# Fetched token rows turned in the odd groups' banks, ahead of the last up product, in a mixture-of-experts kernel

## The reference

```python
D_MODEL = 1024; SEQ = 256; N_EXPERTS = 8; TOP_K = 2; D_FF_EXPERT = 3584

def swiglu(x, wg, wu, wd):
    return (jax.nn.silu(x @ wg) * (x @ wu)) @ wd

def moe_swiglu(xn, router, wg, wu, wd):
    t = xn.reshape(B * S, D)
    logits = (t @ router).astype(jnp.float32)
    top_val, top_idx = lax.top_k(logits, TOP_K)
    gates = jax.nn.softmax(top_val, axis=-1)
    combine = jnp.sum(jax.nn.one_hot(top_idx, N_EXPERTS) * gates[..., None], axis=1)
    out = jnp.zeros_like(t)
    for e in range(N_EXPERTS):
        out = out + combine[:, e:e + 1] * swiglu(t, wg[e], wu[e], wd[e])
    return out
```

## Time and profile before

| what | value |
|---|---|
| median of three runs | 1982.92 us (1981.67 to 1983.06) |
| the profiled execution's own time | 1982.62 us |
| its span in the profile | 1980.8 us |
| mean granted TensorE clock | 0.993 of full speed |
| TensorE busy with matmuls | 97% of the span |
| VectorE busy | 77% |
| ScalarE busy | 62% |
| expert stage | about 517 to 1486 us of the span |

### The profile page before, as it was taken

The page is one execution under the profiler, slowest core; times in us unless marked ns, Lnnn a source line. Parts: engine busy times, 40 slices in busy tenths (PEclk is TensorE's granted clock), DMA queues, the critical chain, the costliest instruction groups (busy, mean ns, idle before and its releaser), DMA issues.

```text
span 1980.8 us, 26870 instructions
## 1 busy us (share of the span) xinstructions
PE 1923.5 (97%) x10275; PEld 1632.1 (82%) x10275; DVE 1518.7 (77%) x1478; ACT 1229.4 (62%) x1332; POOL 28.4 (1%) x28
## 2 busy tenths in 40 slices
PE   8999999999899999999999999999998999999999
PEld 7889998887687887878878788787886788887987
DVE  4675555656788888888888888888996865877576
ACT  4554445554677777777777777777776545354442
POOL 0000000000000000000000000000000000000000
PEclk9999999999999999999999999999999999999999
DMA  7717554532799999999999999999995552345321
GB/s 240 255 59 249 188 192 149 164 113 99 280 375 341 391 379 348 381 340 390 379 348 373 361 395 374 359 384 353 396 361 203 170 171 86 128 170 191 128 86 43
DMA packets 246211, 514.63 MB, mean 260 GB/s; under 512 B 12516, under 2 KB 59240, under 8 KB 246120
## 3 DMA queue, kind: packets, MB, share of 16 engines
q1 hardware_dynamic: 242936, 502.77, 70.4%
q0 software_dynamic: 2896, 10.49, 1.3%
q10 hardware_dynamic: 288, 0.11, 0.0%
HBM read 507.56 MB, written 5.77 MB: 259 GB/s over the span
## 4 chain that ended last, share of the span: by engine, by line
PE 81%; DVE 10%; ACT 3%; issue 3%; SPq 2%; DMA 1%; DVEq 0%; ACTq 0%
PE bank L725 25%; PE bank L727 25%; PE bank L726 25%; DVE low L1936 3%; PE bank L1145 1%; DVE low L2533 1%; PE bank L696 1%; PE bank L849 1%; ACT high L1417 1%; SPq L674 1%; SPq L635 1%; DVE at L2738 1%; PE bank L840 1%; ACT high L1620 1%; PE bank L818 1%
## 5 line engine op out<-in xcount | busy, mean ns | idle before, releaser
L2533 DVE TENSOR_TENSOR low<-raw,high 128x2048 fp32r<-128x2048 f32 x336 | 768.4, 2291 | 117.7 <-ACT high L1620 116.8
L1620 ACT ACTIVATE high<-raw 128x2048 fp32r<-128x2048 f32 x336 | 644.7, 1920 | 240.1 <-PE bank L727 238.3
L1936 DVE TENSOR_TENSOR low<-raw,high 128x2048 fp32r<-128x2048 f32 (+1 forms) x138 | 310.5, 2259 | 168.1 <-ACT high L1417 164.4
L1417 ACT ACTIVATE high<-raw 128x2048 fp32r<-128x2048 f32 (+1 forms) x138 | 260.7, 1894 | 167.8 <-PE bank L727 150.3
L725 PE MATMUL bank<-high,xg_hi 128*128 128x512 f32 x896 | 353.7, 395 | 2.7 <-DVE xg_lo L2516 2.3
L727 PE MATMUL bank<-high,xg_lo 128*128 128x512 f32 x896 | 349.5, 390 | 0.0
L726 PE MATMUL bank<-low,xg_hi 128*128 128x512 f32 x896 | 348.9, 389 | 0.0
L725 PE MATMUL bank<-high,xT_hi 128*128 128x512 f32 (+1 forms) x576 | 228.3, 396 | 8.5 <-issue 5.4
L727 PE MATMUL bank<-high,xT_lo 128*128 128x512 f32 (+1 forms) x576 | 222.2, 386 | 0.0
L726 PE MATMUL bank<-low,xT_hi 128*128 128x512 f32 (+1 forms) x576 | 221.8, 385 | 0.0
L725 PE MATMUL bank<-high,hT_hi 128*128 128x512 f32 x536 | 212.7, 397 | 0.0
(11 more groups left out here) (346 smaller groups left out, 2231.5 us busy)
## 6 DMA issues: line engine op xcount, KB each, us to landing
raw<-in_moe_w_gate SPq DMA_DIRECT2D x112, 1024.0 KB, 6.5
raw<-in_moe_w_up SPq DMA_DIRECT2D x112, 1024.0 KB, 6.8
raw<-in_moe_w_down SPq DMA_DIRECT2D x112, 1024.0 KB, 6.6
raw<-in_w_in SPq DMA_DIRECT2D x63, 1024.0 KB, 5.4
raw<-in_w_out SPq DMA_DIRECT2D x20, 1024.0 KB, 5.0
raw<-in_dense_w_gate SPq DMA_DIRECT2D x11, 1024.0 KB, 5.2
raw<-in_dense_w_up SPq DMA_DIRECT2D x11, 1024.0 KB, 5.3
raw<-in_dense_w_down SPq DMA_DIRECT2D x11, 1024.0 KB, 5.0
```

Of the source, the lines that this page charges most:

```text
L1417: act.activation(high[:, slot, 0:k * n], raw[:, raw_slot[piece], 0:k * n], ACT.Copy).then_inc(high_done, 1)
L1620: act.activation(high[:, k % PARTS, :], raw[:, slot, :], ACT.Copy).then_inc(s["high"], 1)
L1936: dve.tensor_tensor(low[:, slot, 0:k * n], src, high[:, slot, 0:k * n].bitcast(F32), ALU.subtract).then_inc(low_done, 1)
L2533: dve.tensor_tensor(low[:, k % PARTS, :], raw[:, at0 + k % slots, :], high[:, k % PARTS, :].bitcast(F32), ALU.subtract).then_inc(s["low"], 1)
```

## The change

In the pass that fetches rows by DMA (`by_dma`), the eight transposes go into banks 1 and 3, the gate and up banks of the odd groups, and stand ahead of up 6 instead of behind it. They have three semaphores of their own (turned, high, low). The last hidden rows become use 11 of the turning banks, so an expert has 8 uses in place of 10. ACT's `gathered` waits in addition until up 6 has been computed, since it overwrites what up 6 reads. The other pass (for overflowing tokens) and the first and last experts' own lines keep their order.

```diff
-def hidden_at(j, is_last):
-    return 5 + j if j < GROUPS - 1 else (11 if is_last else 13)
+def hidden_at(s, j, is_last):
+    return 5 + j if j < GROUPS - 1 or s["by_dma"] else (11 if is_last else 13)
...
-        moe_sems[0].update(turns=10, by_dma=True)
+        rows_turned, rows_high, rows_low = (sem("taken_rows_" + x) for x in ("turned", "high", "low"))
+        moe_sems[0].update(turns=8, by_dma=True)
...
                         if (what, j) == ("gate", 0):
-                            pe.wait_ge(s["tfree"], 1 + half if is_first else s["turns"] * e + 10 - s["turns"] + half)
+                            if is_first or not s["by_dma"]:
+                                pe.wait_ge(s["tfree"], 1 + half if is_first else s["turns"] * e + 10 - s["turns"] + half)
+                            else:
+                                pe.wait_ge(rows_low, 2 * e - 1 + half)
...
                     if j >= 1:
                         turn_hidden(j - 1)
+                    if j == GROUPS - 1 and not is_last and s["by_dma"]:
+                        turn_taken(e + 1)
                     product("up", j)
...
-                    if j == GROUPS - 1 and not is_last:
-                        if s["by_dma"]:
-                            turn_taken(e + 1, s, lambda a: turn_bank(11 + a))
-                        else:
-                            gather(e + 1, s, lambda a: turn_bank(11 + a))
+                    if j == GROUPS - 1 and not is_last and not s["by_dma"]:
+                        gather(e + 1, s, lambda a: turn_bank(11 + a))
...
                 pe.wait_ge(rows_taken, 16 * e)
                 for a in range(2):
-                    b = bank_for(a)
+                    b = bank[1 + 2 * a]
                     for k in range(4):
                         last = pe.transpose(b[:, k * P:(k + 1) * P], taken_rows[:, (4 * a + k) * P:(4 * a + k + 1) * P],
                                             ident[:, :])
-                    last.then_inc(s["tfull"], 1)
+                    last.then_inc(rows_turned, 1)
...
                     if (what, j, half) == ("up", GROUPS - 1, 1) and not is_last:
-                        gathered(s, s["turns"] * e + 10, (7, 6))
+                        if s["by_dma"]:
+                            act.wait_ge(s["used"], first + PER_EXPERT * e + q + 1)
+                            gathered(rows_turned, 2 * e + 1, rows_high, (1, 3))
+                        else:
+                            gathered(s["tfull"], s["turns"] * e + 10, s["thigh"], (7, 6))
...
                     if (what, j, half) == ("up", GROUPS - 1, 1) and not is_last:
-                        gathered(s, 9 * e + 8, (7, 6))
+                        if s["by_dma"]:
+                            gathered(rows_high, 2 * e, rows_low, (1, 3))
+                        else:
+                            gathered(s["thigh"], 9 * e + 8, s["tfree"], (7, 6))
```

## The result

The changed kernel takes 1969.01 us (median of four runs, 1968.43 to 1971.29), the kernel before in the same comparison 1982.99 us (1981.67 to 1984.22). The ratio is 0.9932, 95% interval 0.9915 to 0.9949. The forecast was 1970.8 us. The profiled execution took 1971.29 us against 1982.62, 11.3 us less.

What follows compares the result with a forecast made beforehand. TensorE, busy 97% of the span, was taken as the bound. Savings of 5.7 + 6.4 = 12.1 us from 1982.62 gave 1970.5, forecast as 1970.8 us since that execution lay 0.3 below the median; range 1967.5 to 1977.5.

Steps and rivals of the forecast that it cites:

- The wait removed and the wait that took its place: At each expert's end, TensorE's 2.07 us wait for `xg_lo` becomes one of 1.37 us before down 6, start to start.
- The cost of the moved transposes: Ahead of up 6 instead of behind it, the eight transposes take the same 0.79 us; their waits add 0.
- The clock: Behind TensorE's waits at the experts' ends, four clock falls of 1.6 us each disappear: 6.4 us gained.
- the bound taken from the earlier trace: Elsewhere, waits of 1.45 and 1.72 us had no clock fall, so the new 1.2 us wait has none.
- Falls stay: Rival at the experts' ends: four clock falls remain, for a cause other than wait length; 1977.2 us, chance 0.1.
- falls everywhere: Rival: seven clock falls in front of down 6 eat the gain; 1982.0 us, no change, chance 0.04.
- The sum: Whole kernel: 5.7 us from seven expert ends plus 6.4 us of clock, 12.1 us gained.
- The stream of weights: Rival inside the experts: the weight stream is the limit, TensorE waits for pieces; time stays 1982.9 us, chance 0.04.
- the late pieces: Behind down 6's start, piece 41's low part is covered by 0.5 us; the next expert's piece 0 is also covered.

Runs made afterwards that it cites:

- The run with the order altered: Changed kernel with VectorE's `low_hidden(6)` placed between the two halves of `xg_lo` instead of behind all eight instructions; 1966.87 us, ratio 0.9931 to the kernel before.
- five cut: Changed kernel with the last five of the eight `xg_lo` instructions each cut into two of 64 columns; 1983.90 us, ratio 1.000 to the kernel before.
- both edits: Changed kernel with the transposes in banks 1 and 3 but behind up 6, and `low_hidden(6)` between the halves of `xg_lo`; 1960.29 us, ratio 0.9892.

## Why the prediction was right

**The wait removed and the wait that took its place.** Right in place, releaser and size. Down 5 starts without the delay behind transposes and ends 2.72 us on; `turn_hidden(6)` starts at once; `low_hidden(6)` starts 6.51 us behind up 6 (1228.30 to 1234.81), as forecast (1238.15 to 1244.66). The wait is 1.33 us start to start, forecast 1.37, and 1.17 as counted, forecast 1.2. The run with the order altered shows that it is VectorE's program order.

**The cost of the moved transposes.** The term "0.79 us ahead of up 6 in place of behind it" is slightly too small. From the transposes of hidden 5 to the end of up 6 it was 5.93 us before (from this row to 870.85)

```profile
864.92 0.60 PE L1145 MATMUL bank<-ident,v 128*128 128x128 f32 x4
```

and is 6.80 us after (1221.50 to 1228.30): 0.87. Behind up 6, the first matmul after the wait starts its successor 0.33 us on in place of 0.23 (1235.54 to 1235.87 in the trace), and down 6 itself started 0.09 us sooner behind up 6 than forecast (7.24 against 7.33), so gate comes 12.81 us behind up 6, forecast 12.77. Together each end gains 0.71 us (121.1 to 120.4) in place of 0.81: 5.0 us, not 5.7.

**The clock.** Four falls of 1.6 us gone, as forecast, 6.4 us. This was the step with the least to rest on, and the runs bear it out at the experts' ends: the number of falls follows the wait's length, with the step between 1.55 and 2.17 us. Two parts of it were luck. The four falls were those of one execution. And the bound taken from the earlier trace rows was a single sight of a place that behaves otherwise in other profiles: there a wait of 2.30 us has no fall behind it in the changed kernel, and one of 1.54 us has one with five cut (rows in the last section). "Falls stay" and "falls everywhere" are both out. The Trainium skill's warning of long gaps alone (TensorE: Matmul & The Clock Gate, "Why this matters for your kernels") would have left the falls in place; the measurement decides against it here.

**The sum.** 5.0 + 6.4 = 11.4 us. From the first expert's first gate matmul to the first matmul behind the last expert's products the profiles show 974.7 us (516.86 to 1491.53) before and 963.6 us (516.69 to 1480.24) after, 11.1 us less; the first end gained 0.2 us less than the next three, with its wait of 1.32 us. The two profiled executions differ by 11.3. The medians differ by 14, and 11.4 lies within the interval of the ratio (10 to 17 us), so the rest may be noise. One possible source the forecast didn't allow for: the falls outside the experts are not the same from run to run. The profile of the changed kernel has one in the first layer, where nothing was changed (a window of TensorE, columns as in the earlier trace rows):

```profile
116.00:120.00 4.00, 4.00 (x19) 0.57 0.02 4
```

Its 1971.29 us is the slowest of the four runs. That this fall is why is not shown: up to the experts the profile took as long as the kernel before's, which has no fall there (516.69 and 516.86 us), and over the ten profiles this stretch lasted from 514.1 to 516.9 us. The kernel before ranged from 1979.12 to 1985.38 us over the runs beside the experiments, some four falls' width. How much of this spread is falls of the clock was not traced run by run.

**The stream of weights and the late pieces.** ScalarE waits for no landed weights in the expert stage after the change either, and with both edits TensorE works without waits at the ends: the stream was no limit even at 119.0 us for each expert. Piece 41 was covered by some 0.6 us (its low part from 1235.40 took 2.28 us, and TensorE wanted it at 1238.39), forecast 0.5, and became the wait as soon as `low_hidden(6)` was sooner.

## What to carry to other kernels

When a wait for a buffer is removed, follow the releasing engine's program on from that point: the next thing in it (here `low_hidden(6)` behind all of `xg_lo`) gives the new wait, and rows of the old trace give its length to 0.05 us. Free the buffer without moving work ahead of the event on which the other engine's chain hangs: the banks without the new place were 5 us better. Count what a wait costs with the clock behind it: at the experts' ends a wait of 1.9 us cost up to 1.6 us more than its length, one of 1.55 us nothing. Find such lengths at the place itself: another place of this kernel showed others.

## What the runs showed of the hardware

At the ends of the experts, in a stretch of matmuls of 512 columns, the clock fell behind none of the waits of 1.17 and 1.55 us, behind some of those of 1.8 to 1.9, behind all of 2.17 and 4.1 and all but one of 2.8. Where ends with and without a fall stand in one profile, a fall cost 1.6 us, behind waits of 1.80, 1.89 and 2.8 us alike.

This is no rule for the whole kernel. At some 50 us, in the first layer's attention, the changed kernel waited 2.30 us and kept its clock; with five cut the same place had a wait of 1.54 us and a fall (line and window of each, columns as in the earlier trace rows):

```profile
52.10 0.94 PE L850 MATMUL bank<-v,probsT 128*128 128x128 f32 x6 [2.30 <-ACT v L1518]
52.00:56.00 4.00, 3.90 (x33) 1.00 1.06 379
```

```profile
50.35 1.51 PE L850 MATMUL bank<-v,probsT 128*128 128x128 f32 x6 [1.54 <-ACT v L1518]
50.00:54.00 4.00, 3.65 (x17) 0.57 1.06 382
```

One fall came behind a wait of 1.09 us only, at 113.68 us in the changed kernel, in a stretch of small matmuls (TensorE busy for 4.82 of 6 us from 110 us); the kernel before had the same wait there and no fall. Behind the experts every profile has a wait of 2.15 to 2.23 us. In nine of the ten the three or four matmuls between it and the next wait run at full clock. The next wait, of 2.9 to 3.6 us, has a fall behind it each time, and such a fall can be longer than those at the ends: in the changed kernel it held twelve matmuls, where those at the ends held some eight.

```profile
1499.27 0.47 PE L726 MATMUL bank<-high,xT_hi 128*128 128x512 f32 x1 [2.17 <-issue]
...
1503.63 0.58 PE L727 MATMUL bank<-low,xT_hi 128*128 128x512 f32 x1 [3.21 <-issue]
1504.02 0.63 PE L728 MATMUL bank<-high,xT_lo 128*128 128x512 f32 x1
```

So the length of a wait orders the ends of the experts, and something more than it decides elsewhere; what that is, no run here tested.

On VectorE, cutting an instruction of 128 columns in two cost about 0.13 us: three cuts lengthened the wait by 0.38 us (1.17 to 1.55).
